# One level of Strassen's product over half the inner dimension of each feed-forward gate/up pair, with the down products taken two pairs at a time

## The reference

```python
h  = rms_norm(x, g)                          # (256, 2048)
hb = silu(h @ w_gate) * (h @ w_up)           # both weights (2048, 5632)
x  = x + hb @ w_down                         # (5632, 2048)
```

## Time and profile before

| | us |
|---|---|
| Three runs | 2114.60, 2114.72, 2115.41 (median 2114.72) |
| Span of the profiled execution | 2112.9 |
| PE busy in it | 2099.0 |
| DVE busy | 1215.2 |
| ACT busy | 902.5 |

### The profile page before, as it was taken

How to read it: one execution, slowest core, us unless ns; L and a number is a source line. 1 busy time by engine, 2 the same in 40 slices (tenths; PEclk the granted TensorE clock), 3 DMA queues, 4 the chain that set the end, 5 groups by cost and what they waited for, 6 DMA issues and landing times.

```text
span 2112.9 us, 24852 instructions
## 1 busy us (share of the span) xinstructions
PE 2099.0 (99%) x10595; PEld 1786.0 (85%) x10595; DVE 1215.2 (58%) x1214; ACT 902.5 (43%) x861; POOL 21.1 (1%) x40
## 2 busy tenths in 40 slices
PE   9999999999999999999999999999999999999998
PEld 8888888888888888888999888888888888888887
DVE  5576555665544544456889755444445454454555
ACT  5444444544343443345353444334333433334443
POOL 2000000000000000000000000000000000000000
PEclk9999999999999999999999999999999999999999
DMA  8655555555555555665655556565555555555553
GB/s 246 224 177 170 177 160 183 176 179 163 196 193 187 198 190 188 199 239 184 205 191 163 179 180 200 183 193 186 199 191 187 187 191 199 186 193 183 194 200 120
DMA packets 224733, 398.34 MB, mean 189 GB/s; under 512 B 11202, under 2 KB 56506, under 8 KB 224368
## 3 DMA queue, kind: packets, MB, share of 16 engines
q1 hardware_dynamic: 221344, 387.64, 56.4%
q0 software_dynamic: 2528, 8.00, 1.2%
q10 hardware_dynamic: 752, 1.12, 0.1%
HBM read 394.62 MB, written 2.12 MB: 188 GB/s over the span
## 4 chain that ended last, share of the span: by engine, by line
PE 95%; DVE 4%; ACT 1%; DMA 0%; issue 0%; ACTq 0%; SPq 0%
PE psA L478 27%; PE psA L480 27%; PE psA L479 27%; PE psA L543 6%; PE psA L547 3%; DVE CA L1464 1%; PE psB L600 1%; DVE lo L1260 1%; DMA X<-in_x_dram 0%; PE psB L698 0%; PE psB L724 0%; PE psB L646 0%; PE psB L758 0%; ACT hi L868 0%; PE psB L685 0%
## 5 line engine op out<-in xcount | busy, mean ns | idle before, releaser
L1260 DVE TENSOR_TENSOR lo<-raw,hi 128x2048 fp32r<-128x2048 f32 (+2 forms) x368 | 834.8, 2272 | 619.8 <-ACT hi L868 617.7
L868 ACT ACTIVATE hi<-raw 128x2048 fp32r<-128x2048 f32 (+2 forms) x368 | 697.9, 1899 | 684.3 <-PE psA L480 592.7
L478 PE MATMUL psA<-hi,XHL 128*128 128x512 f32 x1632 | 637.9, 391 | 0.0
L480 PE MATMUL psA<-hi,XHL 128*128 128x512 f32 x1632 | 633.9, 388 | 0.0
L479 PE MATMUL psA<-lo,XHL 128*128 128x512 f32 x1632 | 633.4, 388 | 0.0
L480 PEld LDWEIGHTS psA<-hi,XHL 128*128 128x128 f32 x1632 | 306.4, 188 | 63.6
L478 PEld LDWEIGHTS psA<-hi,XHL 128*128 128x128 f32 x1632 | 306.5, 188 | 62.6 <-DVE lo L1260 0.4
L479 PEld LDWEIGHTS psA<-lo,XHL 128*128 128x128 f32 x1632 | 306.6, 188 | 61.7
L478 PE MATMUL psA<-hi,YH 128*128 128x512 f32 x608 | 237.2, 390 | 0.0
L480 PE MATMUL psA<-hi,YL 128*128 128x512 f32 x608 | 236.6, 389 | 0.0
L479 PE MATMUL psA<-lo,YH 128*128 128x512 f32 x608 | 236.6, 389 | 0.0
(11 more groups left out here) (353 smaller groups left out, 1273.4 us busy)
## 6 DMA issues: line engine op xcount, KB each, us to landing
raw<-in_w_in_dram SPq DMA_DIRECT2D x158, 1024.0 KB, 5.1
raw<-in_w_gate_dram SPq DMA_DIRECT2D x44, 1024.0 KB, 5.1
raw<-in_w_up_dram SPq DMA_DIRECT2D x44, 1024.0 KB, 5.2
raw<-in_w_down_dram SPq DMA_DIRECT2D x44, 1024.0 KB, 5.1
raw<-in_w_out_dram SPq DMA_DIRECT2D x32, 1024.0 KB, 5.1
raw<-in_w_branch_dram SPq DMA_DIRECT2D x16, 1024.0 KB, 5.0
raw<-in_w_ple_gate_dram SPq DMA_DIRECT2D x16, 1024.0 KB, 5.0
raw<-in_w_in_dram SPq DMA_DIRECT2D x16, 512.0 KB, 4.7
```

The costliest lines, as they stand in the source:

```text
L478: e.matmul(dst, A2[0], B2[0], start=first, stop=False, skip_group_check=True)
L480: return e.matmul(dst, A2[1], B2[0], start=False, stop=last, skip_group_check=True)
L868: e.activation(hi[u % H][:, 0:m], raw[u % R][:, 0:m], ACT.Copy).then_inc(hi_made, 1)
L1260: e.tensor_tensor(lo[u % R][:, 0:m], raw[u % R][:, 0:m], hi[u % H][:, 0:m].bitcast(F32), ALU.subtract).then_inc(lo_made, 1)
```

## The change

The 370 units become 403. Of the gate and the up weights of a slice, the first 8 of 16 blocks of the inner dimension (kb 0 to 7) are multiplied by one level of Strassen's product in Winograd's form: the two token halves, two halves of 4 blocks each and the two column halves (up and gate, 512 columns each) make 2 x 2 blocks, and 7 block products take the place of 8. The other 8 blocks (kb 8 to 15) are multiplied as before.

One group `S` for each slice has 11 units, `STEPS` = a, x, p2, f, p3, e, d, p0, c, g, p1. The seven one-letter units are the Strassen products, of 12 matmuls each (4 blocks, three matmuls); p0 to p3 are plain quarters of the inner dimension, of 24 matmuls each. The weights a and c (up) and b and d (gate) are loaded. DVE makes from them the combinations x = b - a, f = d - x, g = c - f and e = d - b (`form` in the DVE's `mixed`, 128x2048 each, e written over b), which ACT and DVE then split like loaded weights. The matching combinations of the input (S1 to S4) are made once (`input_forms`, at unit 214) and split into `SFH`, `SFL`. Partial results are taken out of PSUM while the group runs: ACT copies four quarters of `psA` (P1 into `S1B` after a, P5 into the second half of `CG` after x, U2 after f, U3 after e), and DVE adds the rest (`gate_up`, `hidden`).

The downs are taken for two slices at a time, so there are six rounds in place of three; two of their banks lie in `psB`. There are eight `raw` buffers in place of five and five `hi` buffers in place of four; buffers 5 and 6 lie in the memory of `YH` and `YL` and are free from unit 218 on. `fills` gives every load and every combination the buffer that comes free first. From unit 210 on the splits run four units ahead. `lo` still overwrites `raw`.

```diff
-R = 5
-H = 4
+R, MORE_R = 5, 3
+H, MORE_H = 4, 1
 AHEAD = 3
+FURTHER = 210
...
+STEPS = ("a", "x", "p2", "f", "p3", "e", "d", "p0", "c", "g", "p1")
+SOURCE = {"a": (0, 0), "b": (1, 0), "c": (0, 4), "d": (1, 4), "p0": (0, 8), "p1": (0, 12), "p2": (1, 8), "p3": (1, 12)}
+FILLED = ("a", "b", "x", "d", "f", "p2", "c", "g", "p3", "p0", "p1")
+FORMS = {"x": 1, "f": 2, "e": 3, "g": 4}
+BANKS = ({"A": 0, "B": 3, "C": 1, "D": 2}, {"A": 1, "B": 0, "C": 2, "D": 3})
...
+    def mixed(j):
+        g = Group(len(groups), ("S", j), "S", (A["w_up_2"][0], A["w_gate_2"][0]), 512 * j, STEPS, len(units))
+        groups.append(g)
+        for i in range(len(STEPS)):
+            units.append((g, i))
+
     def down(js, turn):
+        four = []
         for f in range(4):
-            group(("down", 4 * turn + f), "N", A["w_down_2"][0], 512 * f,
-                  [[(4 * j + k, 4 * (j % 4) + k) for k in range(4)] for j in js])
-
-    for j in range(11):
-        group(("fg", j), "N", A["w_gate_2"][0], 512 * j, K16)
-        if j in (4, 8):
-            down(range(j - 4, j), j // 4 - 1)
-        group(("fu", j), "N", A["w_up_2"][0], 512 * j, K16)
+            g = Group(len(groups), ("down", 4 * turn + f), "N", A["w_down_2"][0], 512 * f,
+                      [[(4 * j + k, 4 * (j % 2) + k) for k in range(4)] for j in js], len(units))
+            groups.append(g)
+            four.append(g)
+        order = [(f, i) for two in ((0, 1), (2,), (3,)) for i in range(len(js)) for f in two]
+        for f, i in order:
+            four[f].last = len(units)
+            units.append((four[f], i))
+
+    for j in range(0, 10, 2):
+        mixed(j)
+        mixed(j + 1)
+        down((j, j + 1), j // 2)
+    mixed(10)
     for f in range(4):
         group(("proj", f), "N", A["w_ple_proj_2"][0], 512 * f, [[(0, 0), (1, 1)]])
-    down((8, 9, 10), 2)
+    down((10,), 5)
     for f in range(4):
...
+def fills(units):
+
+    free = [(0, n) for n in range(R)] + [(206, 7), (218, 5), (218, 6)]
+    hfree = [(0, n) for n in range(H)] + [(206, 4)]
+    landed = [0] * (R + MORE_R)
+    places, loads = {}, []
+    hplaces = []
+
+    def take(key, until, W=None, k0=0, nk=4, pieces=()):
+        free.sort()
+        after, slot = free.pop(0)
+        if W is not None and len(loads) >= 2:
+            landed[slot] += 16 * len(pieces)
+        places[key] = (slot, after, landed[slot])
+        free.append((until + 1, slot))
+        if W is not None:
+            loads.append(Fill(places[key], W, k0, nk, pieces))
+
...
+                if role == "a":
+                    if j == 0:
+                        e.wait_ge(flip_low, SECOND + 1)
+                        e.wait_ge(bank_dve, freed(("out2", LOWER)))
+                    elif j % 2:
+                        e.wait_ge(*gate(j - 1, "t0"))
+                    else:
+                        e.wait_ge(bank_dve, freed(("down", 2 * j - 2)))
+                    x = block("A", 0, t0, first=True)
+                elif role == "x":
+                    if j == 0:
+                        e.wait_ge(sf_low, 1)
+                    elif j % 2:
+                        e.wait_ge(*gate(j - 1, "t1"))
+                    x = form("C", 1, first=True)
+                elif role == "p2":
+                    if j == 0:
+                        e.wait_ge(flip_low, SECOND + 3)
+                        e.wait_ge(bank_dve, freed(("out2", 5 - LOWER)))
+                    elif j % 2:
+                        e.wait_ge(*up(j - 1, "t0"))
+                    block("D", 8, t1, first=True)
+                    e.wait_ge(*copied(j, "P5"))
+                    x = block("C", 8, t0)
+                elif role == "f":
+                    e.wait_ge(*copied(j, "P1"))
+                    x = form("A", 2)
+                elif role == "p3":
+                    if j == 0:
+                        e.wait_ge(flip_low, SECOND + 4)
+                    block("D", 12, t1, last=True)
+                    x = block("C", 12, t0)
+                elif role == "e":
+                    e.wait_ge(*copied(j, "U2"))
+                    x = form("A", 3)
+                elif role == "d":
+                    x = form("C", 4, last=True)
+                elif role == "p0":
+                    if j % 2:
+                        e.wait_ge(*up(j - 1, "t1"))
+                    block("B", 8, t0, first=True)
+                    e.wait_ge(*copied(j, "U3"))
+                    x = block("A", 8, t1)
+                elif role == "c":
+                    x = block("B", 4, t0)
+                elif role == "g":
+                    x = block("A", 4, t1)
+                else:
+                    block("B", 12, t0, last=True)
+                    x = block("A", 12, t1, last=True)
...
                 g, i = units[u]
-                m = g.width * len(g.parts[i])
-                e.wait_ge(raw_landed[u % R], landed[u])
-                if u >= H:
-                    e.wait_ge(unit_done, u - H + 1)
-                e.activation(hi[u % H][:, 0:m], raw[u % R][:, 0:m], ACT.Copy).then_inc(hi_made, 1)
+                m = UNIT if g.kind == "S" else g.width * len(g.parts[i])
+                slot, _, landed = place(u)
+                hslot, after = hplaces[u]
+                if g.kind == "S" and STEPS[i] in FORMS:
+                    e.wait_ge(form_made, 4 * g.name[1] + FORMS[STEPS[i]])
+                else:
+                    e.wait_ge(raw_landed[slot], landed)
...
+            def mixed(u):
+
+                g, i = units[u]
+                role, j = STEPS[i], g.name[1]
+                if role == "a":
+                    e.wait_ge(unit_done, u + 1)
+                    if j:
+                        e.wait_ge(*up(j - 1, "hidden"))
+                    else:
+                        e.wait_ge(sf_low, 1)
+                    e.activation(S1B[:, :], quarter(j, "A"), ACT.Copy).then_inc(sum_copied, 1)
+                elif role == "x":
+                    e.wait_ge(unit_done, u + 1)
+                    if j:
+                        e.wait_ge(*up(j - 1, "hidden"))
+                    e.activation(CG2, quarter(j, "C"), ACT.Copy).then_inc(sum_copied, 1)
+                elif role == "f":
+                    e.wait_ge(unit_done, u + 1)
+                    e.activation(CG1, quarter(j, "A"), ACT.Copy).then_inc(sum_copied, 1)
+                elif role == "e":
+                    e.wait_ge(unit_done, u + 1)
+                    e.activation(SU3[:, :], quarter(j, "A"), ACT.Copy).then_inc(sum_copied, 1)
+                elif role == "p0":
+                    e.wait_ge(*gate(j, "t1"))
+                    e.wait_ge(ffn_scales, 1)
+                    e.activation(THF[:, 512:1024], CG2, ACT.Tanh, scale=hr2[:, 1:2])
+                elif role == "c":
+                    e.wait_ge(*gate(j, "t0"))
+                    e.activation(THF[:, 0:512], CG1, ACT.Tanh, scale=hr2[:, 0:1]).then_inc(fg_tanh, 1)
...
             for u in range(n_units):
+                g, i = units[u]
                 side(u)
-                if 0 < u < n_units - AHEAD and u not in ATTEND and u not in EARLY:
-                    split(u + AHEAD)
-                g, i = units[u]
-                if u == g.last:
+                if g.kind == "S" and STEPS[i] == "x":
+                    mixed(u)
+                if u and u not in ATTEND and u not in EARLY:
+                    for n in ahead(u):
+                        split(n)
+                if u == SUMS:
+                    e.wait_ge(sf_sum, 1)
+                    e.activation(SFH[:, :, :, :], SS[:, :, :, :], ACT.Copy).then_inc(sf_high, 1)
+                if g.kind == "S":
...
+                def form(dst, p, q):
+                    slot, after, _ = places[j, dst]
+                    if dst != "b":
+                        e.wait_ge(unit_done, after)
+                    e.tensor_tensor(of[dst], of[p], of[q], ALU.subtract).then_inc(form_made, 1)
...
+                if role == "a":
+                    arrived("a")
+                    arrived("b")
+                    form("x", "b", "a")
+                elif role == "x":
+                    arrived("d")
+                    e.wait_ge(form_made, 4 * j + 1)
+                    form("f", "d", "x")
+                elif role == "f":
+                    arrived("c")
+                    e.wait_ge(form_made, 4 * j + 2)
+                    form("g", "c", "f")
+                split(u)
+                if role == "p2":
+                    form("b", "d", "b")
+
+            def gate_up(u):
+
+                g, i = units[u]
+                role, j = STEPS[i], g.name[1]
+                if role == "d":
+                    e.wait_ge(*copied(j, "U3"))
+                    e.wait_ge(*copied(j, "P5"))
+                    finish(e.tensor_tensor(CG2, CG2, SU3[:, :], ALU.add))
+                    e.wait_ge(unit_done, g.first + STEPS.index("p3") + 1)
+                    e.tensor_tensor(CG2, CG2, quarter(j, "D"), ALU.add).then_inc(gate_made, 1)
+                elif role == "p0":
```

(35 more changed lines are left out.)

289 lines of the change are left out of this document (213 added, 76 removed).

## The result

| | us |
|---|---|
| Before, four runs beside the change | 2114.60 to 2115.41, median 2114.80 |
| The change, four runs | 2151.10 to 2159.38, median 2154.61 |
| Ratio | 1.0190, 95% interval 1.0173 to 1.0206 |

The change makes the kernel slower by 39.8 us. The range of the prediction holds the time, and the sign is the one forecast. The forecast, 2141, is 13.6 us short. The profiled execution is the slowest of the four (2159.38, mean granted clock 0.987); the two fastest (2151.1 and 2151.7) ran at 0.990 and 0.991.

A forecast was written before the change was run, and what follows sets the result against it. PE was taken to bound the kernel. Saved matmuls (-29.9 us) and new waits (49.8) gave +19.9, clock falls +6.6: 2114.7 + 19.9 + 6.6 = 2141 us, range 2118 to 2161.

The forecast's parts named there:

- -29.9 us for 132 matmuls: PE runs 12 matmuls fewer in each of 11 slices, at 0.2267 us each: -29.9 us.
- Place 1: Second half of p2, slices 2, 4, 6, 8, 10: PE waits 2.9 us each for ACT's copy of P5.
- Place 2: Head of p2, slices 1, 3, 5, 7, 9: PE waits 4.5 us each for DVE's add of S1B.
- Place 3: The opening: the flip before p2 waits 12.1 us for DVE's adds of the last out2 into X.
- The second wait there, 0.7: The opening, first slice: PE waits 0.7 us more in p2 until ACT has copied P5 out.
- The clock, +6.6: The granted clock falls at the opening and the five long gaps, 6 x 1.1 = +6.6 us.
- upper bound of 2.3: Most that one fall of the granted clock costs the matmuls after a gap: 2.3 us; the least is 0.
- Flips elsewhere cost nothing: Outside the opening: as many flips as before, 0.9 us of PE each, and no other waits.
- B: Rival: the clock falls at every gap, 11 falls at up to 2.3 us, 2160 us; chance 0.18.
- C: Rival: loads at all three places land in 3.6 us, not 5.1, 2118 us; chance 0.07.
- D: Rival: waits at places 1 and 2 don't bind, only the opening is paid, 2098 us; chance 0.09.
- E: Rival: DVE falls behind, combinations take 4.6 us, over 2180 us; chance 0.06.

The follow-up runs named there:

- e9: e8 with 12 matmuls put back in each slice, their results thrown away: 2124.71 us, ratio 1.0046 to the kernel before.
- e1: The change with ACT's copy of P1 put ahead of the split of p3: 2151.89 us, ratio 1.0172 to the kernel before.
- e5: The change with ACT's copies of P1 and P5 both ahead of the split of p3: 2135.25 us, ratio 1.0096 to the kernel before.
- e2: The change with DVE making the hidden slice ahead of combination g and split f: 2141.24 us, ratio 1.0123 to the kernel before.
- e7: e6 with DVE adding the last out2 quarter ahead of the splits of p2 and f in the opening: 2100.61 us, ratio 0.9931.
- e3: The change with PE running 50, 18 or 11 matmuls, results thrown away, ahead of the eleven waits: 2141.62 us, ratio 1.0126 to the kernel before.
- e4: The kernel before with only the downs changed, taken two slices at a time, the last round with one slice: 2121.83 us, ratio 1.0031.
- e8: e7 with ACT summing squares after the turned quarter's high part in the last downs: 2095.15 us, ratio 0.9905 to the kernel before.
- e6: The change with the edits of e5 and e2 together: 2106.01 us, ratio 0.9955 to the kernel before.

## Why the prediction was right, and where it was short

- **-29.9 us for 132 matmuls: right.** The page counts 132 fewer, and e9 measures 29.6, within some 3 us.
- **Place 1, 5 x 2.9: right in place, partner and chain**, measured 2.48 to 2.79 (13.4 against 14.5). e1 and e5 show that what stands ahead of P5's copy makes the wait.
- **Place 2, 5 x 4.5: right**, 4.15 to 4.58, with DVE's row of operations as counted. e2 shows that the order of DVE is the cause: the wait goes without DVE doing less.
- **Place 3, 12.1: right**, 11.95, and e7 removes it by order alone. The second wait there, 0.7, did not show. It would have hung on P5's copy in slice 0, after a stretch in which PE ran at 1.2 GHz and so came later itself; that this covered it was not tried by itself.
- **The clock, +6.6: too small, the step that failed.** The prediction let it fall at the opening and the five long gaps at 1.1 each. It fell at nine gaps, and each cost 2.1 on the mean (1.3 to 3.0). The prediction's upper bound of 2.3 was worked out wrongly: half of the 5.2 us that it read from the earlier trace rows is 2.6, and some falls cost more than either. Nothing spoke for the middle between the bounds. Together 18.5 in the profiled execution; e3 takes away 18.0, of which 1.1 lie at the start. Gaps of 2.48 and 2.73 us passed without a fall, others of 2.68 to 2.79 didn't.
- **Flips elsewhere cost nothing: wrong by 4.4 us**, the second step that failed. The prediction took the downs' adds and banks into account, but not the flips of `X` behind the last round, which had three slices' work between them and now have one. e4 has the loss alone, and e8 removes it by moving the squares.
- **Small ones, not in the sum:** 1.1 at the start of the program, where the clock rose later than in the profile before, 2.2 for the drawn ends, and 1.2 left open.

Together: 2141 + 11.9 (clock) + 4.4 (flips) + 3.3 (start and drawn ends) - 2.6 (places a little shorter) = 2158.0, against 2159.4 of the profiled execution. The median lies 4.8 below that one, and the granted clocks say why: two of the four runs had less of its loss (0.990 and 0.991, not 0.987).

**The rivals.** *B* (every gap, 2160) has the clock's mechanism nearly whole, 9 of 11 and 2.1 of 2.3 (with 2.6 it would have given 2163); the time lies nearer to it than to the forecast, and its chance of 0.18 was too low. *C* is out: the loads between 1290 and 1940 us landed 4.9, 5.1 and 6.7 us after their issue (least, median, most), none near 3.6, and the two shown at places 1 and 3 took 5.2 and 5.1. *D* is out by the waits. But e6 is the kernel that *D* described, with no wait at places 1 and 2 and the opening paid: it took 2106.0 where *D* gave 2098, and of the 8 us between, the late flips are 4.4 and the fall of the clock at the opening 2.2. *E* is out: 33 combinations of this form took 2281 to 2293 ns each, as much as a split:

```profile
L1555 DVE TENSOR_TENSOR raw<-raw x33: 2281/2284/2293, 1255.5 to 1969.3; 128x2048 f32<-128x2048 f32 x33
```

## What to carry to other kernels

When an algorithm saves work on the engine that sets the time, that engine may come to wait for new small operations of the others, and an engine that takes its program in order does these behind whatever is listed first. Here copies out of PSUM stood behind a split that waited for a load, and 132 matmuls saved turned into 39.8 us lost; the same instructions in another order gained 20.1. Ask of each new operation for which PE will wait what stands ahead of it, and whether the foremost waits for a transfer; average busy shares (DVE 66%, ACT 46%) say nothing of it. Count a gap in PE's work of 4 us or more at its length plus about 2 us for the clock, as measured here, and a gap between 2.3 and 3.2 us as one that may or may not cost that.

## What the runs showed of the chip

- The length of a gap alone doesn't decide whether the clock falls. In the change part of the work behind a gap of 4.15 to 4.58 us ran at 1.2 GHz in five of five cases (e1 and e5, 4.27 to 4.59: ten of ten), behind one of 2.48 to 2.79 in three of five. In e1 a gap of 2.26 us was followed by a fall (0.79 over the next 8 us), in e2 one of 2.98 was not (1.00). And the same gap of the opening went both ways, in e7 and in e8:

```profile
1281.52 0.50 PE L608 MATMUL psA<-hi,XHL 128*128 128x512 f32 x1 [3.22 <-DVE lo in YH L1540]
1281.52:1289.52 8.00, 7.12 (x30) 5.60 (x31) 8.00 (x4) 7.84 (x12) 0.00 (x0) 1.00 0.61 206
...
1281.96 0.79 PE L608 MATMUL psA<-hi,XHL 128*128 128x512 f32 x1 [3.17 <-DVE lo in YH L1541]
1281.96:1289.96 8.00, 8.00 (x23) 6.34 (x24) 8.00 (x4) 7.82 (x12) 0.00 (x0) 0.62 0.50 183
```

  No run here tells what else decides. The Trainium skill, TensorE: Matmul & The Clock Gate, section "Why this matters for your kernels", warns of gaps between bursts of matmuls. The rows of 4.15 us and more agree; the shortest gap with a fall here, 2.26 us, is shorter than those of which the page warns, and there the measurement decides. e3 puts the price of the change's nine falls at 13 to 18 us.
- Matmuls that nobody needs are a remedy where a wait can't be taken away: 195 of them (50 + 5 x 18 + 5 x 11; the page of e3 has 10658 matmuls) made e3 13.0 us faster than the change, in time in which PE would have been idle.
